# Attention stages of a two-block transformer: inverse softmax sums turned in 64-row halves among the probability transposes, and modulation rows turned behind the value products in 64-column halves

## What is computed

```python
mod = c_silu @ ada_w + ada_b                      # layer 0 and, for layer 1, spread over the attentions
s = jnp.einsum('bqhgd,bkhd->bhgqk', qi, k_all)
p = softmax_f32(s, v_all.dtype)                   # exp(s - max) / sum
y = jnp.einsum('bhgqk,bkhd->bqhgd', p, v_all)
ux = jnp.concatenate([ya, yb, yc_], axis=-1) * jax.nn.silu(px[9])
```

## Time and profile before

| what | value |
|---|---|
| median of 3 runs | 1854.64 us (1851.79 to 1855.0) |
| the profiled execution | 1852.03 us, its span 1850.2 us |
| PE busy | 1817.2 us, 98% of the span |
| DVE, ACT busy | 1261.6 us (68%), 1083.4 us (59%) |
| chain that ended last | PE 92%, ACT 3%, DVE 2% |
| PE clock | granted in full but for short stretches |

### The profile page before, as it was taken

How to read it: one execution, slowest core, us unless ns; L and a number is a source line. 1 busy time by engine, 2 the same in 40 slices (tenths; PEclk the granted TensorE clock), 3 DMA queues, 4 the chain that set the end, 5 groups by cost and what they waited for, 6 DMA issues and landing times.

```text
span 1850.2 us, 34397 instructions
## 1 busy us (share of the span) xinstructions
PE 1817.2 (98%) x13400; PEld 1577.4 (85%) x13400; DVE 1261.6 (68%) x2157; ACT 1083.4 (59%) x1907; POOL 55.0 (3%) x57
## 2 busy tenths in 40 slices
PE   7999999999999999999999999999999999999998
PEld 5878878879888978889889988889888889998887
DVE  6663354478726678776686787757776677688765
ACT  5372264385736487764656577746774556567762
POOL 0000000003000000001000000000000000000001
PEclk9999999999999999999999999999999999999999
DMA  9232243242234315555432445554554642355553
GB/s 356 101 115 84 98 157 112 92 145 98 86 113 143 118 67 182 192 194 208 182 115 92 173 179 194 181 199 173 191 187 173 220 156 93 137 182 182 182 184 134
DMA packets 42571, 285.49 MB, mean 154 GB/s; under 512 B 4944, under 2 KB 6352, under 8 KB 9424
## 3 DMA queue, kind: packets, MB, share of 16 engines
q1 hardware_dynamic: 40832, 278.24, 41.9%
q0 software_dynamic: 1616, 5.52, 0.9%
HBM read 282.69 MB, written 1.05 MB: 153 GB/s over the span
## 4 chain that ended last, share of the span: by engine, by line
PE 92%; ACT 3%; DVE 2%; issue 1%; DMA 1%; SPq 0%; POOL 0%; DVEq 0%; ACTq 0%
PE bank L2340 25%; PE bank L2334 14%; PE bank L2335 13%; PE bank L2336 13%; PE bank L2341 13%; PE bank L2607 3%; PE bank L2553 3%; PE bank L2521 2%; PE bank L2438 1%; ACT work L1101 1%; PE bank L2508 1%; DMA token_major<-weights 1%; DVE panels_lo L1508 1%; ACT token_major L1079 1%; PE bank L2535 1%
## 5 line engine op out<-in xcount | busy, mean ns | idle before, releaser
L2340 PE MATMUL bank<-acts,panels_hi 128*128 128x512 f32 x2032 | 710.6, 396 | 0.5 <-DVE panels_lo L1508 0.5
L1508 DVE TENSOR_TENSOR panels_lo<-raw_panels,panels_hi 128x1024 fp32r<-128x1024 f32 x468 | 573.0, 1242 | 188.2 <-ACT panels_hi L954 186.5
L954 ACT ACTIVATE panels_hi<-raw_panels 128x1024 fp32r<-128x1024 f32 x468 | 484.4, 1054 | 248.3 <-PE bank L2336 152.5
L2341 PE MATMUL bank<-acts,panels_lo 128*128 128x256 f32 x2032 | 565.3, 278 | 0.0
L2340 PEld LDWEIGHTS bank<-acts,panels_hi 128*128 128x128 f32 x2032 | 381.3, 188 | 91.6 <-DVE panels_lo L1508 1.3
L2341 PEld LDWEIGHTS bank<-acts,panels_lo 128*128 128x128 f32 x2032 | 382.2, 188 | 0.1
L2334 PE MATMUL bank<-acts,panels_hi 128*128 128x256 f32 (+1 forms) x1120 | 350.9, 313 | 1.1 <-DVE xT L1587 0.4
L2335 PE MATMUL bank<-acts,panels_hi 128*128 128x256 f32 (+1 forms) x1120 | 345.8, 309 | 0.0
L2336 PE MATMUL bank<-acts,panels_lo 128*128 128x256 f32 (+1 forms) x1120 | 345.7, 309 | 0.0
L2334 PEld LDWEIGHTS bank<-acts,panels_hi 128*128 128x128 f32 x1120 | 213.4, 191 | 18.1 <-issue 4.5
L2336 PEld LDWEIGHTS bank<-acts,panels_lo 128*128 128x128 f32 x1120 | 213.5, 191 | 10.8
(11 more groups left out here) (304 smaller groups left out, 1868.7 us busy)
## 6 DMA issues: line engine op xcount, KB each, us to landing
raw_panels<-weights SPq DMA_DIRECT2D x252, 1024.0 KB, 4.8
token_major<-weights SPq DMA_DIRECT2D x4, 1024.0 KB, 9.0
near_bias<-rpb POOLq DMA_DIRECT2D x12, 256.0 KB, 3.7
xT<-xin SPq DMA_DIRECT2D x4, 512.0 KB, 5.6
gates<-weights SPq DMA_DIRECT2D x2, 1024.0 KB, 10.1
near_bias<-weights SPq DMA_DIRECT2D x4, 512.0 KB, 7.3
token_major<-weights SPq DMA_DIRECT2D x2, 512.0 KB, 12.6
token_major<-rpb POOLq DMA_DIRECT2D x4, 256.0 KB, 2.8
```

The costliest lines, as they stand in the source:

```text
L954: act.activation(slot_hi(n, a, b), raw_of(n, a, b), ACT.Copy).then_inc(hi_ready, 1)
L1508: dve.tensor_tensor(slot_lo(n, a, b), raw_of(n, a, b), slot_hi(n, a, b).bitcast(F32), ALU.subtract).then_inc(lo_ready, 1)
L2340: pe.matmul(bank.rearrange("p (c t) -> p c t", c=2), whi_, with_rest(xhi_), start=start, stop=False, skip_group_check=True)
L2341: return pe.matmul(bank[:, 0:T], wlo_, xhi_, start=False, stop=stop, skip_group_check=True)
```

## The change

Steps of which the spread is moved are those that have a deferred step behind them in the same attention: 60 of the 68. There the one 128x128 transpose for each 128 queries (76 of 88 in all) becomes two transposes of 64 rows. The first (rows 0 to 63) stands behind the first pair of the second head's transposes, the other (rows 64 to 127) behind the last. Both write bank 6, and a new semaphore, `half_spread`, which PE increments itself, makes each wait until the one before is done; the waits for `normed` and `omul` now stand ahead of the first half, inside the transposes. The last step of each attention keeps its whole spread. `to_columns` for the 16 modulation rows that are turned within the attentions goes behind the value products, and each of its two products becomes two of 64 columns. `out_bank` becomes a function that returns the same bank 6.

```diff
-        def to_columns(rows, dst):
+        def to_columns(rows, dst, width=P):
 
             for e in range(2):
-                o = pe.matmul(dst[:, 2 * e:2 * e + 2], rows[:, e * P:(e + 1) * P], const("sel"),
-                              start=True, stop=True, skip_group_check=True)
+                for c in range(0, P, width):
+                    o = pe.matmul(dst[c:c + width, 2 * e:2 * e + 2], rows[:, e * P + c:e * P + c + width], const("sel"),
+                                  start=True, stop=True, skip_group_check=True)
...
+            def spread(j, h):
+
+                rows = slice(h * HD, (h + 1) * HD)
+                for k, q0 in steps[j].deferred:
+                    a = T + q0 + h * HD
+                    o = pe.transpose(out_bank(blk, st, steps[j].pair)[:, a:a + HD], inverse_rows(blk, g0 + j, k)[rows],
+                                     ident[rows, h * HD:(h + 1) * HD])
+                return o
...
-                        for c, d in un.blocks:
+                        for n, (c, d) in enumerate(un.blocks):
                             turn_probs(g, e, c, d, 0)
                             o = turn_probs(g, e, c, d, 1)
+                            if e and n == 0 and j and steps[j - 1].deferred:
+                                out_bank_free(j - 1)
+                                if halves.n:
+                                    pe.wait_ge(half_spread, halves.n)
+                                spread(j - 1, 0).then_inc(half_spread, 1)
                     o.then_inc(probT, 1)
+                    if j and steps[j - 1].deferred:
+                        pe.wait_ge(half_spread, halves.n + 1)
+                        spread(j - 1, 1).then_inc(half_spread, 1)
+                        halves.n += 2
...
-                    else:
+                    elif j == len(steps) - 1 or not step.deferred:
                         out_bank_free(j)
-                        for k in range(len(step.deferred)):
-                            whole_spread(j, k)
+                        if step.deferred:
+                            whole_spread(j)
```

More of the change, by code:

```diff
@@ L385, in program @@
     near_hi = sem("near_queries_keys_hi")
+    half_spread = sem("inverses_turned_by_half")
     scores, negmax, exped, normed = sem("scores"), sem("negmax"), sem("exped"), sem("probs_normed")
@@ L751, in turned_to, with out_bank @@
         return x.rearrange("p e (b h q) -> p h e b q", h=2, q=HD)
-    out_bank = banks[6]
+    def out_bank(blk, st, pair):
+        return banks[6]
     def late_bank(m, l):
@@ L1702, in attention @@
                     dve.wait_ge(gate_last_out, late)
-                    dve.scalar_tensor_tensor(y, out_bank[:, T:2 * T], 0.5, gate_of(1, pairs[-1]), ALU.mult,
+                    dve.scalar_tensor_tensor(y, out_bank(blk, st, steps[j].pair)[:, T:2 * T], 0.5, gate_of(1, pairs[-1]), ALU.mult,
                                              ALU.mult).then_inc(last_weighed, 1)
@@ L1707, in attention @@
                     dve.wait_ge(last_weighed, 1)
-                    dve.tensor_tensor(y, out_bank[:, 0:T], y, ALU.mult).then_inc(omul, 1)
+                    dve.tensor_tensor(y, out_bank(blk, st, steps[j].pair)[:, 0:T], y, ALU.mult).then_inc(omul, 1)
                 elif 0 <= j < len(steps) and steps[j].last:
@@ L1713, in attention @@
                         dve.wait_ge(usplit, now(usplit, p0 + pr - 1))
-                    y = gated(p0 + pr)
+                    y, bank = gated(p0 + pr), out_bank(blk, st, pr)
                     if late and pairs[pr][0] == NPAIR - 1:
                         dve.wait_ge(gate_last_out, late)
-                        m = dve.scalar_tensor_tensor(y, out_bank[:, 0:T], 0.5, gate_of(1, pairs[pr]), ALU.mult, ALU.mult)
+                        m = dve.scalar_tensor_tensor(y, bank[:, 0:T], 0.5, gate_of(1, pairs[pr]), ALU.mult, ALU.mult)
                     elif blk == 1:
-                        m = dve.tensor_tensor(y, out_bank[:, 0:T], gate_of(1, pairs[pr]), ALU.mult)
+                        m = dve.tensor_tensor(y, bank[:, 0:T], gate_of(1, pairs[pr]), ALU.mult)
                     else:
-                        m = dve.tensor_copy(y, out_bank[:, 0:T])
+                        m = dve.tensor_copy(y, bank[:, 0:T])
                     if steps[j].deferred:
@@ L1724, in attention @@
                         dve.wait_ge(dve_chain, chain.next())
-                        m = dve.tensor_tensor(y, out_bank[:, T:2 * T], y, ALU.mult)
+                        m = dve.tensor_tensor(y, bank[:, T:2 * T], y, ALU.mult)
                     m.then_inc(omul, 1)
@@ L2509, in turn @@
             o.then_inc(turned, 1)
+        halves = Chain(half_spread)
         def attention(blk, mixer, with_ctx, st, ahead):
@@ L2530, in out_bank_free, with whole_spread @@
                     pe.wait_ge(normed, now(normed, 2 * (g0 + j) + 2))
-            def whole_spread(j, k):
-                q0 = T + steps[j].deferred[k][1]
-                pe.transpose(out_bank[:, q0:q0 + P], inverse_rows(blk, g0 + j, k), ident)
+            def spread(j, h):
[5 more added lines that the diff above has]
+                return o
+            def whole_spread(j):
+                for k, q0 in steps[j].deferred:
+                    o = pe.transpose(out_bank(blk, st, steps[j].pair)[:, T + q0:T + q0 + P], inverse_rows(blk, g0 + j, k), ident)
+                return o
             for i in range(len(steps) + 3):
@@ L2583, in attention @@
                         branch_gate(st, r)
[L2584 to L2589, removed]
                 j = i - 3
@@ L2603, in attention @@
                         pr = pairs[step.pair][0]
-                        pe.matmul(out_bank[:, 0:T], vblk[:, pr * P:(pr + 1) * P], pcT, start=True, stop=False,
+                        pe.matmul(out_bank(blk, st, step.pair)[:, 0:T], vblk[:, pr * P:(pr + 1) * P], pcT, start=True, stop=False,
                                   skip_group_check=True)
                     for k, (e, v, c, n, q0, start) in enumerate(step.adds):
-                        o = pe.matmul(out_bank[e * HD:(e + 1) * HD, q0:q0 + n], v, probsT(g)[:, c:c + n],
+                        o = pe.matmul(out_bank(blk, st, step.pair)[e * HD:(e + 1) * HD, q0:q0 + n], v, probsT(g)[:, c:c + n],
                                       start=start, stop=k >= len(step.adds) - 2, skip_group_check=True)
@@ L2610, in attention @@
                 if far_tail and j == len(steps) - 2:
-                    g = g0 + len(steps) - 1
-                    pe.wait_ge(normed, 2 * g + 2)
-                    pe.transpose(out_bank[:, T + P:2 * T], inverse_rows(blk, g, 0), ident).then_inc(last_inverse, 1)
+                    pe.wait_ge(normed, 2 * (g0 + len(steps)))
+                    whole_spread(len(steps) - 1).then_inc(last_inverse, 1)
+                for r, slot in enumerate(ADA_SLOTS[mixer] if st.panels and blk == 1 else ()):
+                    row = ADA_ROW[mixer] + r
+                    if i == slot + 2:
+                        pe.wait_ge(row_out, row + 1)
+                        c = MOD_COLS + 4 * row
+                        to_columns(cmpw[:, 0:PW], banks[7][:, c:c + 4], HD).then_inc(row_turned, 1)
                 if blk == 1 and i >= len(steps):
```

## The result

The changed kernel takes 1861.97 us as a median of 6 runs (1861.4 to 1863.38) beside 1854.27 (1849.67 to 1855.15) for the kernel before: a ratio of 1.0046, 95% interval 1.0036 to 1.0056. It is 7.7 us slower, and the forecast of no change, with its range up to 1858.7, was wrong.

The account below looks back on a forecast made before the run. PE's order was taken to bound layer 0, with PE, ACT and DVE close together in layer 1. Gains of 1.7 and 2.1 less losses of 0.2 and 3.8 gave 0.2 us lost: no change, 1854.6 us, range 1850.0 to 1858.7.

Parts of the forecast that it names:

- the paragraph on late inputs: In 20 moved steps PE would wait for DVE's gating at the first half, losing 0.33 - a each; 3.8 us net.
- Four MoBA spreads with inputs ready: With two transpose pairs behind the first half, the wait outweighs the drain: 0.03 to 0.09 us lost each, 0.2 in all.
- rival "clock": Longer PE stalls bring one more stretch at half clock, about 1.7 us; chance 0.01, together with any other slower case.
- The ready step: Values start 0.55 us after the pair ahead of the first half, not 0.60; single and double steps gain 1.7 us.
- the faster rival: PE's wait on its own semaphore costs nothing, values start at 0.465 us; 4.6 us gained, 1850.0; chance 0.25.
- the account by the drains alone: One of two tiling-mode drains leaves each of 60 moved steps, 0.15 us each: 9 us gained, 1845.6; chance 0.02.
- Waits and signals: Exposed increments on PE's products add 3.1 us, 1857.7, or waits 0.05 us dearer in 60 steps add 3.0; chance 0.04.
- The rows: Modulation rows turned behind the values: 0.27 us gained per row on a ready step, 2.1 us over all rows.
- The rival on the columns: The rows' half passes do not run side by side or cost as much as whole ones: 3.8 us more, 1858.6; chance 0.04.
- Late steps of the first block: Moved steps with late gating, mostly first of a pair: twelve lose 0.27 to 0.30 us, five 0.13 to 0.2, part hidden.
- The rival "slower, by ACT": In three layer 1 steps PE's signal to ACT waits behind DVE, delaying ACT's copy and exponentials: 1858.7 us; chance 0.08.
- The signs of the forecast: Trace signs: values at 0.55 us, second half 0.04 to 0.06 after the first, PE's waits for DVE from 3.6 to some 7.

Follow-up runs that it names:

- e1: The changed kernel with MoBA's steps spread whole and in their old place, the first block as changed: 1854.12 us, ratio to before 1.0005.
- e2: The kernel before with only MoBA's waits moved inside the transposes, spreads whole and in place: 1860.51 us, ratio 1.0040.
- e4: The changed kernel with the one MoBA step per layer whose values follow a gate panel spread whole as before: 1854.16 us.
- e6: The kernel before with MoBA's waits moved, plus three unread 128x256 products ahead of the wait in the gate-panel step: 1859.74 us, ratio 1.0039.
- e3: The kernel before with only the modulation rows turned behind the values in 64-column halves: 1850.03 us, ratio 0.9985.
- e5: The changed kernel with halves only in the first block's steps that are not first of a pair, rows as changed: 1847.58 us; repeated, 1849.99 us.
- e9: The kernel before, unchanged, run and profiled again: 1852.37 us.
- e7: The changed kernel, MoBA as before, halves in layer 1 and layer 0's second steps, layer 1's pairs alternating between two banks: 1846.15 us, ratio 0.9967.

## Why the prediction was wrong

**The failed step** is the paragraph on late inputs: "If DVE's gating ends a us before the old spread, and a is under 0.33", applied to all 60 steps, together with "Four MoBA spreads with inputs ready ... 0.2 in all". The limit of 0.33 holds where the spread follows the transposes directly. In the MoBA step of each layer at 1022.2 and 1599.2 a gate panel of 5.85 us stands between the two. There the wait moved ahead by 6.1 us, not by 0.34. The gating, 4.3 us ahead of the old spread, looked ready and was 1.8 us late for the new place. The description of the kernel says that a gate panel stands there; for the modulation rows the same reasoning was done (0.46 us of cover) and for the panel it was left out. In place of 0.2 the four steps cost 7.1 us; e1, e2 and e4 show it from three sides. (The counts of that part, 31, 4, 4 and 20 steps, make 59 of the 60.)

**The second size** was the clock, which is no term of the sum. The rival "clock" had it as one drop more, 1.7 us, with a chance of 0.01 that it comes with another of the slower cases; it came in both gate steps, at 1.5 us each (e2 against e6), and, by the mean clocks of e1 and e3, in the first block besides.

**What held.** The ready step: values 0.55 us after the pair ahead of the first half were forecast, and 98.79 - 98.25 = 0.54 came. So the faster rival fell, which had 0.465, and so did the account by the drains alone, with its 0.15 a step: 0.06 us were gained in this step (0.60 before), 0.036 a step over the 20 of e5. Waits and signals that cost 0.05 more a step did not come either. The rule of the Trainium skill behind the drains (TensorEngine Tiling (Array Packing), section Key Properties: changing the tiling mode drains the engine) agrees with the trace, in which the old spread starts 0.15 us after the last pair of transposes and the pairs are 0.06 apart, but it is not all that a step pays.

The rows: 2.1 forecast, 2.6 measured in e3 (0.45 gone before the values, 0.18 to 0.19 added behind them). The rival on the columns fell with them: the 64-column halves do run side by side, their eight records begin within 0.15 us. Late MoBA steps: 0.29 each, as worked out.

**What held only in part.** Late steps of the first block: halves there were to cost 3.7 - 0.5 - 1.7 = 1.5 us net; e4 against e3 gives 2.0, but the medians of e1 and e3 give 4.1, with what the clock adds. That the first block came out even, as in the sum, is therefore in part luck: a gain and a loss both larger than forecast. The rival "slower, by ACT" did not occur at its price: PE's waits for ACT fell from 3.6 to 2.3 us. But one late step of layer 1 cost 1.0 us in place of 0.3. In the kernel before, its values started 0.96 us after the first of the transposes (490.19 and 491.15), where a ready step needs 0.85; in e1 it is 1.97 (487.63 and 489.60):

```profile
489.07 0.27 PE L2542 MATMUL bank<-consts_sb,token_major 64*128 64x64 f32 x1 [0.91 <-DVE work L1727]
```

The trace of e1 shows where this came from, from two iterations earlier on:

```profile
482.55 0.27 PE L2542 MATMUL bank<-consts_sb,token_major 64*128 64x64 f32 x1 [1.00 <-DVE work L1727]
...
483.05 1.02 ACT L1081 ACTIVATE token_major<-bank 128x1024 f32<-128x1024 f32 x1 [1.46 <-PE bank L2526]
...
483.97 1.05 ACT L956 ACTIVATE panels_hi<-raw_panels 128x1024 fp32r<-128x1024 f32 x1
...
485.06 1.23 DVE L1510 TENSOR_TENSOR panels_lo<-raw_panels,panels_hi 128x1024 fp32r<-128x1024 f32 x1 [0.96 <-ACT panels_hi L956]
```

The first late half spread holds back the signal of the transposes. ACT stands idle for 1.46 us before its copy (0.30 in the kernel before) and rounds the panel half late, DVE waits 0.96 us for that half (in the kernel before it does not wait there), and its next gating is late for PE. This is the path of the rival, the signal to ACT behind the wait for DVE; it came back to PE through DVE's panel half and gating, not through the exponentials. No run takes it apart.

The signs of the forecast were nearly right: waits for DVE were to grow "to some 7 us", and in e1, without MoBA, they are 7.1. The rest, to 11.4, is the gate steps and a later neighbour.

## What to carry to other kernels

When a wait is moved ahead, measure its slack against the new place, for every instance of the loop, and list what stands between the old and the new place there: two steps of sixty with a long job in between cost more than all the others together could gain. Move the waiting work only where its inputs are ready (here the second step of each pair), and try the parts of a compound change one by one: the rows alone gain 3.3 us, which the steps with late inputs and the two MoBA steps buried. A standstill of 1.6 us on PE cost about twice its length here, since the clock dropped behind it; filling it with idle products mended that step and not the time of the program.

## What was not expected of the hardware

The first feed-forward stage runs at one of two paces, without any wait and at full granted clock. Two windows from 720 to 840 us, of the kernel before and of the same program in e9:

```profile
720.00:840.00 120.00, 120.00 (x694) 104.93 (x693) 93.80 (x127) 79.91 (x116) 0.00 (x0) 1.00 0.54 190
```

```profile
720.00:840.00 120.00, 120.00 (x681) 104.13 (x680) 93.83 (x127) 79.82 (x115) 0.00 (x0) 1.00 0.51 183
```

694 against 681 products in 120 us, all of the same two shapes, and the starts of successive pairs are 346.7 or 353.3 ns apart. Over the stage that is 3.0 us. The faster pace came in the profiles of before, e3, e5 and e7, the slower in the other eight, e5 repeated among them. It goes with the execution and not with the program, and it is as large as most of the effects studied here. What chooses it was not tried. PE's clock also fell to half for 3.4 us at places that differ between executions of one program (125.3 and 930.8 us in before, 933.8 in e9), once where PE was busy throughout (e6, 1512).
